# Changing the order of three instruction queues at the end of each attention slot: inverse sums, next tile's row work, and value products

## The reference, cut to what matters

```python
p_mla, p_rwkv, p_conv = _split(h @ w_in, [MLA_PROJ, RWKV_PROJ, CONV_PROJ])
# head group A: latent attention; the sampled part goes over a paged cache
s_past = einsum('bqhc,bkc->bhqk', q_lat, ckv_past) + einsum('bqhr,bkr->bhqk', q_rope, kr_past)
pr = softmax(concatenate([s_past, s_new]) * ATTN_SCALE)
out = einsum('bhqk,bkc->bqhc', pr[..., :n_past], ckv_past) + ...
# head group B: RWKV-7, one state S per head, step by step over the tokens
sa = einsum('bhvk,bhk->bhv', s, -kk_t)
s  = s * w_t + sa * (kk_t * a_t) + v_t * k_t
y  = einsum('bhvk,bhk->bhv', s, r_t)
# head group C: a short convolution; then w_out, layer norm, 32 experts (2 per token), layer norm
```

## Time and profile before

| | us |
|---|---|
| median of 3 runs | 2915.4 (2912.5, 2915.8, 2915.4) |
| the profiled execution | 2936.7 |
| its span, first to last instruction | 2934.7 |
| TensorE busy in the span | 2673.3 (91%) |
| VectorE busy | 1247.3 (43%) |
| ScalarE busy | 833.8 (28%) |
| GpSimd busy | 744.0 (25%) |

### The profile page before, as it was taken

How to read it: one execution, slowest core, us unless ns; L and a number is a source line. 1 busy time by engine, 2 the same in 40 slices (tenths; PEclk the granted TensorE clock), 3 DMA queues, 4 the chain that set the end, 5 groups by cost and what they waited for, 6 DMA issues and landing times.

```text
span 2934.7 us, 55370 instructions
## 1 busy us (share of the span) xinstructions
PE 2673.3 (91%) x22106; PEld 1439.4 (49%) x22106; DVE 1247.3 (43%) x3354; ACT 833.8 (28%) x2025; POOL 744.0 (25%) x808
## 2 busy tenths in 40 slices
PE   7999889999999959999599998999999996799996
PEld 4445566666655523333244456666666454233332
DVE  4213665555543542222451255565554446222224
ACT  0111455555532001111101015555555210011113
POOL 1000322221110035555310002322211000555543
PEclk9999999999999969999799999999999997899998
DMA  8212434332242539998751133343322326599985
GB/s 300 73 35 56 157 108 119 100 100 92 74 142 90 234 139 347 374 359 313 251 212 48 38 112 123 110 116 120 97 90 76 130 77 252 208 370 355 334 307 207
DMA packets 171810, 502.19 MB, mean 171 GB/s; under 512 B 48388, under 2 KB 89608, under 8 KB 146344
## 3 DMA queue, kind: packets, MB, share of 16 engines
q1 hardware_dynamic: 105624, 321.28, 31.7%
q0 software_dynamic: 50240, 120.23, 12.0%
q10 hardware_dynamic: 15696, 57.15, 4.9%
HBM read 629.15 MB, written 86.89 MB: 244 GB/s over the span
## 4 chain that ended last, share of the span: by engine, by line
PE 78%; DVE 9%; ACT 3%; another core or an unknown queue 3%; DMA 3%; issue 2%; DVEq 2%; POOL 0%; POOLq 0%; ACTq 0%; SPq 0%
PE ps L1011 70%; PE ps L1008 8%; ACT PT L1974 1%; DVE grams L2543 1%; DVE S_all L3022 1%; DMA xd<-o_x 1%; DMA ybd<-yb 1%; ACT S_all L2275 1%; DMA l_b<-ybd,dga 0%; ACT grams L1974 0%; DVE PT L3052 0%; DMA c_x<-xd 0%; DVE krT L3044 0%; DVE uu L2543 0%
## 5 line engine op out<-in xcount | busy, mean ns | idle before, releaser
L1011 PE MATMUL ps<-w_slots,xbT 128*64 128x512 f32 (+1 forms) x2048 | 461.7, 604 | 19.0 <-DVE xbT L3465 19.0
L1011 PE MATMUL ps<-hT,w_in 128*128 128x512 f32 x896 | 392.0, 595 | 1.2 <-ACT hT L1974 1.2
L912 POOL DMA_INDIRECT xb<-xd,idall x256 | 256.9, 1004 | 145.0 <-issue 81.0
L1011 PEld LDWEIGHTS ps<-w_slots,xbT 128*64 128x64 f32 x2048 | 144.5, 139 | 290.9 <-issue 271.4
L1011 PEld LDWEIGHTS ps<-hT,w_in 128*128 128x128 f32 x896 | 167.8, 190 | 203.4 <-issue 200.0
L1011 PE MATMUL ps<-w_out,o_mixT 128*128 128x512 f32 (+1 forms) x640 | 243.4, 561 | 1.3 <-DVE o_h L3271 1.3
L1011 PE MATMUL ps<-w_slots,hidT 128*64 128x512 f32 (+1 forms) x1024 | 233.6, 596 | 8.5 <-issue 6.9
L3465 DVE STREAM_TRANSPOSE xbT<-xb 128x1024 f32<-128x1024 f32 x64 | 79.7, 1245 | 323.2 <-DMA xb<-xd,idall 316.2
L818 POOL TENSOR_TENSOR lnt<-lnt,cst 128x1 f32<-128x1 f32 x36 | 37.3, 1037 | 518.6 <-DVE lnt L2552 518.6
L1011 PE MATMUL ps<-grams 64*64 64x64 f32 (+1 forms) x3536 | 140.7, 225 | 27.3 <-DVE grams L2543 24.8
L1011 PE MATMUL ps<-kcat,qcat 96*128 96x512 f32 (+3 forms) x384 | 151.6, 503 | 5.9 <-DVE low L3022 5.9
(11 more groups left out here) (444 smaller groups left out, 4157.8 us busy)
## 6 DMA issues: line engine op xcount, KB each, us to landing
w_slots<-in_w_gu SPq DMA_DIRECT2D x64, 2048.0 KB
w_slots<-in_w_dn SPq DMA_DIRECT2D x64, 1024.0 KB
ybd<-yb ACTq DMA_DIRECT2D x64, 512.0 KB
pd<-stage SPq DMA_DIRECT2D x56, 256.0 KB, 2.5
w_in<-in_w_in SPq DMA_DIRECT2D x6, 2048.0 KB, 24.3
out_y<-c_h ACTq DMA_DIRECT2D x18, 512.0 KB, 3.3
o_mixT<-mixd SPq DMA_DIRECT2D x18, 512.0 KB, 4.0
xd<-o_x ACTq DMA_DIRECT2D x18, 512.0 KB, 2.9
```

The source lines that it names most:

```text
L912: pool.indirect_dma_start(xb[p % 2][:, 256 * q:256 * q + 256], None, x_quarters, bass.IndirectOffsetOnAxis(ap=idall[:, NE * q + p:NE * q + ...
L1011: return pe.matmul(out, lhsT, rhs, start=start, stop=stop, skip_group_check=True)
```

## The change

No instruction is added or removed; five places of the written order are changed.

1. PE, end of slot: `off3` goes ahead of `mv`, directly behind `scores(0)`.
2. PE, end of slot: the value products `v(0)` and `v(1)` stand directly behind `scores(1)` and `scores(2)`, ahead of `u(0)` and `u(1)`.
3. ACT, end of slot: the next tile's `th` and `ssq` go from behind `off1` to behind `both(2)`.
4. DVE, end of slot: `off2` goes ahead of `s(0)`; `off3`, `sg` and `ssx` go ahead of `max(0)`, `off3` first.
5. DVE, slots 1 to 7: `ropes(0)` and `ropes(1)` go ahead of `rr(2)`, and `t.a()` goes behind it.

```diff
-DVE_ATT = "1s0 1s1 1s2 1s3 1s4 1s5 1s6 1s7 1rden 1a 2r0 2r1".split()
+DVE_ATT = "1s0 1s1 1s2 1s3 1s4 1s5 1s6 1s7 1rden 2r0 2r1 1a".split()
...
-ACT_SEAM = "2th 2ssq 1off2 1mv 1wt 1u0 2kk 1u1 1y 2lora 2cq 2mlaT 2gate 2qn 2exps 2kn 2V 2qrT 2tokm".split()
-DVE_SEAM = ("1off2 2sg 2ssx 1off3 2rows 1st0 1st1 2kkx 2logs 2qr 2kk2 2rkv").split()
+ACT_SEAM = "1off2 2th 2ssq 1mv 1wt 1u0 2kk 1u1 1y 2lora 2cq 2mlaT 2gate 2qn 2exps 2kn 2V 2qrT 2tokm".split()
+DVE_SEAM = ("1off2 1off3 2sg 2ssx 2rows 1st0 1st1 2kkx 2logs 2qr 2kk2 2rkv").split()
...
@@ PE, end_of_slot
                 b.scores(0)
+                x.off3()
                 x.mv()
-                x.off3()
                 b.both(3)
                 x.wt()
                 b.both(4)
                 b.scores(1)
+                b.v(0)
                 x.u(0)
-                b.v(0)
                 b.both(5)
                 x.st(0)
                 b.both(6)
                 b.scores(2)
+                b.v(1)
                 x.u(1)
-                b.v(1)
                 b.both(7)
                 x.st(1)
@@ ACT, end_of_slot
                 x.off1()
                 if sample:
                     sample.mixT()
-                y.th()
-                y.ssq()
                 b.both(1)
                 x.off2()
                 b.both(2)
+                y.th()
+                y.ssq()
                 x.mv()
@@ DVE, end_of_slot
                 x.off1()
+                x.off2()
                 b.s(0)
-                x.off2()
-                b.max(0)
+                x.off3()
                 y.sg()
                 y.ssx()
-                x.off3()
+                b.max(0)
                 b.turned(0)
@@ DVE, slot
                 t.rden()
+                b.ropes(0)
+                b.ropes(1)
+                x.rr(2)
                 t.a()
-                b.ropes(0)
-                x.rr(2)
-                b.ropes(1)
                 end_of_slot(x, y, b)
```

More of the change, by code:

```diff
@@ L187 @@
 DVE_SATT = "s0 m0 T0 s1 m1 r2 o0 T1 s2 m2 r3 o1 T2 s3 m3 o2 T3 o3".split()
-DVE_ATT = "1s0 1s1 1s2 1s3 1s4 1s5 1s6 1s7 1rden 1a 2r0 2r1".split()
+DVE_ATT = "1s0 1s1 1s2 1s3 1s4 1s5 1s6 1s7 1rden 2r0 2r1 1a".split()
 DVE_SATT0 = "r0 r1".split()
-PE_A = ("2gramD 2gram23 2sq0 2gram4 2rr0 1mixT 2sq1 2rr1 2sq2 2rr2 2off1 2off2 2mv 2off3 2wt "
+PE_A = ("2gramD 2gram23 2sq0 2gram4 2rr0 1mixT 2sq1 2rr1 2sq2 2rr2 2off1 2off2 2off3 2mv 2wt "
         "2u0 2st0 2u1 2st1").split()
 PE_S = ("q kkb qlat qrT tokm gramD gram23 new sq0 gram4 rr0 sq1 rr1 sq2 rr2 off1 off2 mv off3 wt").split()
-PE_S0 = ("2mlaT 2lora 1u0 2kks 2q 2kkb 2kn 2V 1y2 2qrT 1st0 2tokm 2gramD 2gram23 2sq0 2gram4 2rr0 2sq1 2rr1 2sq2 2rr2 2off1 1mixT 2off2 2mv 2off3 2wt "
+PE_S0 = ("2mlaT 2lora 1u0 2kks 2q 2kkb 2kn 2V 1y2 2qrT 1st0 2tokm 2gramD 2gram23 2sq0 2gram4 2rr0 2sq1 2rr1 2sq2 2rr2 2off1 1mixT 2off2 2off3 2mv 2wt "
          "2u0 2st0 2u1 2st1").split()
```

## The result

| | before | after |
|---|---|---|
| median of 5 runs, us | 2915.8 (2912.5 to 2925.4) | 2870.1 (2866.9 to 2877.4) |
| ratio, 95% interval | | 0.9837 (0.9816 to 0.9858) |
| span of the profiled execution | 2934.7 | 2866.6 |
| the same two kernels in a later session, medians | 2917.2 | 2872.5, ratio 0.9842 (0.9825 to 0.9859) |

The time fell by 45.7 us. The forecast was 2880, 36 less, with 2871 as the range's lower end: the direction and the mechanism came out, the size did not.

A forecast was written before the change was run, and what follows sets the result against it. TensorE, 91% busy, was taken to bound the kernel; removing its slot-end waits gives 38 us, less 2 for thin covers, so 2915.4 - 36 = 2879, say 2880 us. Range 2871 to 2903, the forecast's own 2873 to 2888 (0.72).

The forecast's parts named there:

- What bounds the kernel: Whole kernel: TensorE busy 91% of the span and 78% of the last-ending chain, so time saved in slots leaves the end.
- the chain has no transfer: From the first slot to the end of the output products, either layer: what follows a slot waits only for the slot.
- The places of the waits and what ends them: TensorE at slot ends: off1 0.78 us, both(2) 0.37, off3 0.66, wt 0.82, together 2.63, removed by reordering VectorE, ScalarE and TensorE.
- Starts, not brackets: TensorE's waits at slot ends: start-to-start distances give 2.63 us, printed brackets 2.30; 38 us against 33 in the sum.
- The covers: Slot ends: moved work stays hidden, with 0.3 to 1.5 us to spare; 2 us taken off for covers perhaps too thin.
- The step that failed: v(0) and v(1) ahead of u(0) and u(1) on TensorE: saves 0, could cost 0.7 us per chunk.
- The sum: All slots: 31.6 us in slots 1 to 6, 3.6 in slots 7, 2.9 in first slots; 38 together, 36 after deduction.
- The rivals: Half the gain returns, 2898 us (0.17); waits move to the seam, about 2914 (0.06); slower, 2940 (0.05).
- the third one: v(0) and v(1) block TensorE's queue waiting for T0 and T1 behind lengthened VectorE operations: 2940 us, chance 0.05.
- From the profile to the runs: Whole time: median of runs 0.7% below the profiled execution, so the 36 us gain times 0.993 stays 36.

The follow-up runs named there:

- the single edits: Kernel before with one piece alone; stretch of seven slots, 481.5 us before: edit 5 475.88, edit 3 479.63, edits 1 and 4 470.15, edit 2 479.42.
- The second profile: Kernel before, unchanged, profiled again: slots 481.41 and 481.85 us, experts 369.1 and 361.5 us in the two layers; its one run took 2913.8 us.

## Why the prediction was wrong, point by point

- **What bounds the kernel**: right. All of the gain that the two profiles agree on lies in the slots and their output stretch, and the 44 us that went there left the end. One reading was wrong and cost nothing: "the chain has no transfer" up to the end of the output products. It has one among them in each layer, from o_x to xd, 12.04 and 11.19 us; the changed kernel has both too (10.46 and 10.69), and the gain of the slots passed through.
- **The places of the waits and what ends them**: right, all four. Per slot, forecast and measured by the single edits: off1 0.78 and 0.80; both(2) 0.37 and 0.31; off3 and wt 0.66 + 0.82 = 1.48 and 1.59, of which 0.14 is no wait but the like shapes of off3 and mv (the run without edit 1), which leaves 1.45. Here slot 1 was not typical: wt's bracket is 0.75 there, and 0.66, 0.66, 0.89, 0.67, 0.66 and 0.66 in the other slots of 0 to 6.
- **"Starts, not brackets"**: right. For the stretch of seven slots the forecast's terms give 7 x (0.78 + 0.66 + 0.82) + 6 x 0.37 = 18.0 us by starts and 7 x (0.71 + 0.59 + 0.75) + 6 x 0.25 = 15.9 by brackets. The run without edit 2 is shorter than before by 18.5, by TensorE's starts by 18.3; less 7 x 0.14 = 1.0 for the shapes, the waits were worth 17.3. Starts are 4% off, brackets 8%; both(2), put at 0.37, gave 0.31.
- **The covers**: right. T0 had its 1.4 us, uu and mv's copies were in time, nothing was delayed by a() or by the rope transposes. So the 2 us that I took off for thin covers were a mistake of their own.
- **The step that failed is edit 2**: "TensorE does the same products, so nothing goes by itself ... I take 0; below, the edit could save nothing". It saves 0.30 us a slot, 16 x 0.30 = 4.8 us, because v's weights load 0.46 us behind the scores' and u's 0.99. I bounded it only by waits; the order of instructions also sets how soon a weight load can start under the matmuls ahead. The same oversight left out 16 x 0.14 = 2.2 us of edit 1.
- **The sum**: 38 + 4.8 + 2.2 - 0.06 x 12 (both(2)) = 44.3, against 44.3 us by the stretches and 45.7 and 44.7 by the medians. That the first two agree to 0.1 is luck: the stretches leave out what lies ahead of the first mark, and the output stretch alone varies by 2 us. With the 2 us taken off, the forecast was 36. The range's lower end, 44 us below before, allowed only for less than the sum and little more, though one edit's cost had been bounded from one side.
- **The rivals**: none happened. What the third one needed, long small operations on VectorE, did come, but too few and too short. The new order puts ssx beside a fetch of rotary keys on POOL (L874) more often: in the changed kernel's first profile 4 such ssx took 0.27 to 0.41 us, in its second 2, in the kernel before one and none, and all others 0.15 to 0.18. T0's 1.4 us to spare covered them; TensorE waits for PT nowhere but once a layer, 1.25 us at the end of slot 7, and the kernel before does so too.
- **From the profile to the runs**: scaling by 0.993 did no harm, but the 21 us between the profiled execution of before and the median were not spread evenly. The second profile shows where they lay: 16 us in the experts, 5 in the output products, none in the slots, so a gain in the slots needs no scaling.

## What to carry to other kernels

Where one engine is 91% busy and its short waits repeat, add them up start to start, with the spacing of the same group where nothing stops it; a sum of such waits, each with its own cause, came out within 4% here. When you reorder instructions on TensorE, count also which weight shapes become neighbours: moving a group beside one of the same shape was worth 0.14 us each time, with no wait involved. And the place of a 0.4 us operation on a half-idle engine can be worth 1 us a slot if it stands behind eleven others that nobody needs yet.

## What the runs showed of the hardware that was not expected

- Behind matmuls with weights of 128 rows and 32 columns (512 columns wide), the next weights went in 0.46 us behind the last ones when they had the same shape, and 0.99 to 1.00 us behind with 64x64, 64x128 or 32x32; the next group's start moved from 0.99 to 0.88. It hangs on the shape and not on the part of the array: with the parts reversed it stayed 0.88. For 64x64 behind 64x64 the next group started after 0.52 us instead of 0.61.
- The Trainium skill (TensorE: Matmul & The Clock Gate, "The mechanism") says that a weight load is pulled ahead of running matmuls when it goes to other rows of the array or to the background buffer, and further down that it overlaps only where the rows differ. Here v's weights use all 128 rows, as the scores' do, and were loaded early; and u's, of half the rows, were not. The second sentence is not borne out in these traces.
- The experts' stretch, which no edit touches, varied between 360 and 376 us a layer over the 14 profiled executions, more than edits 2 and 3 are worth together: for changes of this size the repeating stretch in the trace tells what the median of a few runs can't.
